# Splitting the operand transposes at the five residual boundaries of a six-block transformer kernel

## The chip, the cores and the metric

The kernel runs on one core of one Trainium2 chip, as one program with one launch. The time is the device time of an execution in microseconds (us). The profile is one execution recorded by the hardware profiler; its span runs from the first to the last instruction. The span of a profiled execution is a little shorter than its device time, because some work lies around it.

## The reference, cut to what matters

Input `x` is 256 tokens by 1024 features, float32. Six blocks follow each other, and each adds to the residual stream `h`:

```
h = x
h = h + dsa_mixer(rms_norm(h, a_attn_norm), a_w_in, ...) @ a_w_o      # tag wo
h = h + square(relu(rms_norm(h, mlp_norm[0]) @ up[0])) @ down[0]      # M0
h = h + mla_mixer(rms_norm(h, ...), latent weights w_dq, w_dkv) @ b_w_o   # B, tag bo
h = h + square(relu(rms_norm(h, mlp_norm[1]) @ up[1])) @ down[1]      # M1
h = h + (gated mLSTM and dilated attention of rmsnorm(h) @ w_in_2) @ w_out_2  # C, tag co
h = h + (silu(hf @ w_gate) * (hf @ w_up)) @ w_down,  hf = rmsnorm(h)  # F
out = rmsnorm(h, norm_final_g)
```

## The kernel before, in words

**Precision.** Every float32 operand is kept as a high part (rounded to fp32r) and a low part (the rest). The helper `three` (L546 to L550) issues three matrix products for each pair: high by high, high by low, low by high. Weights come in chunks of up to 1 MB. For each chunk c, SP loads it into one of two raw buffers, ACT makes the high part (`split_one`, L1566), and DVE (L2125) or POOL (L1535) makes the low part. There are three buffers for the parts, so ACT's split of chunk c waits until PE has finished chunk c-3 (`chunk_done`). SP's load of chunk c waits until the low part of chunk c-2 is made. Each engine has its own hand-written instruction order; semaphores tie them together.

**The boundary between two blocks.** There are five boundaries of one form: wo to M0, M0 to B, bo to M1, M1 to C, and co to F. The residual product of a block (tokens by 1024 features) fills four PSUM banks, called quarters 0 to 3: quarter = 2 * token block + feature half. Of its last chunk, PE does six products per quarter, in the order 0, 1, 2, 3 (`down_products`, L589), and closes each bank. DVE adds each quarter to `hres` (`residual_add`, L2131, instructions at L2138 and L2141). PE then turns `hres` to feature-major form with 16 transposes in four banks (`late_transposes`, L658, instruction L668): features 0 to 511 (half 0) need quarters 0 and 2, features 512 to 1023 (half 1) need quarters 1 and 3. ACT makes the high part of each of the eight feature tiles k (L1613; L1813 for B) and DVE the low part (L2151; L2402 for B). Tiles 0 to 3 come from half 0, tiles 4 to 7 from half 1. Within ACT's `late_norm`, tile k+2 waits for the low part of tile k. The next block's first products read these tiles. The scale by the root of the mean square is applied later, from squares of `hres` that ACT sums after the eight tiles (L1552).

**What stands around it.** After the products of tag wo and bo, the four quarters lie in banks 2 to 5; `mlp` waits for banks 4 and 5 to be read (`for b in (4, 5)`, L694) before its first product writes them. At M0 to B, ACT splits chunk `dkva` (L1812, `split_to("dkva")`) ahead of the first feature tile; three chunks before `dkva` stands the last down chunk of M0, whose `chunk_done` is the close of quarter 3. At M1 to C, ACT splits chunk `qm0` after the squares and roots, and DVE makes its low part next; PE needs it for `conv_tile(0)`, right after the matmuls of `C.rs` (L1151). At B, PE's first chunk (`dqa`) does nine products for each k, at C (`vm0a`) PE does token block 0 for all k and then token block 1.

```
for half in range(2):
    for blk in range(NB):
        wait_read(f"{tag}.res{2 * blk + half}")
    for odd in range(2):
        ...
```

Of the kernel before, what the change touches and what calls it, by code (L numbers as in the profile page):

```python
# [23 lines left out]
P = 128  # L24
SEQ = 256
NB = SEQ // P
D = 1024
KT = D // P
# [80 lines left out]
def program(nc, t):  # L109
# [8 lines left out]
    with ctx:  # L118
# [408 lines left out]
        def _(pe):  # L527
# [61 lines left out]
            def down_products(c, xh, xl, start, stop, closing, skip=False, base=0, quarters=(0, 1, 2, 3)):  # L589

                hi, lo = slot(c, 2, D)
                for blk in range(NB):
                    for half in range(2):
                        if 2 * blk + half not in quarters:
                            continue
                        for k in range(2):
                            ins = three(psum[:, base + 2 * blk + half, :], xh(k, blk), xl(k, blk),
                                        hi[:, k, half * 512:half * 512 + 512], lo[:, k, half * 512:half * 512 + 512],
                                        start and k == 0, stop and k == 1, skip)
                        if closing:  # L600
                            close_bank(ins, closing[2 * blk + half])
                return ins
# [24 lines left out]
            def residual(tag, x, ready):  # L627
                open_residual(tag)
                for j in range(4):
                    residual_step(tag, j, x, ready)  # L630
# [27 lines left out]
            def late_transposes(n, tag):  # L658

                for half in range(2):  # L660
                    for blk in range(NB):
                        wait_read(f"{tag}.res{2 * blk + half}")
                    for odd in range(2):
                        k0 = 4 * half + odd
                        out = open_bank(f"{n}.xT{2 * half + odd}", late_bank[n][2 * half + odd])
                        for i, k in enumerate((k0, k0 + 2)):
                            for blk in range(NB):
                                ins = nc.tensor.transpose(out[:, (2 * i + blk) * P:(2 * i + blk) * P + P],  # L668
                                                          hres[:, blk, k * P:k * P + P], ident[:, :])
                        close_bank(ins, f"{n}.xT{2 * half + odd}")  # L670
# [18 lines left out]
            def mlp(i):  # L689

                n = f"M{i}"
                late_transposes(n, ("wo", "bo")[i])
# [5 lines left out]
                def up_step(c, s_count, lo_count, j2, ready=None):  # L698
# [5 lines left out]
                    for nt in range(2):  # L704
                        out = psum[:, 4 + 2 * j2 + nt, :]
                        for k in range(KT):
                            if ready and nt == 0:
                                ready(k)
                            nc.tensor.matmul(out, hi[:, k, nt * P:nt * P + P], xA[:, :, k, :], start=k == 0, stop=False)  # L709
                            ins = nc.tensor.matmul(out[:, 0:SEQ], lo[:, k, nt * P:nt * P + P], xA[:, 0, k, :],  # L710
                                                   start=False, stop=k == KT - 1)
                    ins.then_inc(up_full, 1)

                def down_step(c, h_count, lo_count, j3, start, last):
# [3 lines left out]
                    ins = down_products(c, lambda k, blk: hb[:, 0, k, blk * P:blk * P + P],  # L718
                                        lambda k, blk: hb[:, 1, k, blk * P:blk * P + P],
                                        start, True, names if last else None, True)  # L720
                    if not last:
                        ins.then_inc(down_done, 1)
# [5 lines left out]
                up_step(c0, None, low[c0], 0, late_tile(n))  # L728
# [21 lines left out]
                down_step(c, b0 + NM, low[c], (NM - 1) % 3, False, True)  # L750

            def attention(L, logits, vcol, tag, between):
# [56 lines left out]
                for j in (2, 3):  # L809
                    product(j, (0, 1, 2, 3))  # L810
# [156 lines left out]
            late_transposes("B", "M0")  # L967
            outs = [open_bank(f"B.z{nt}", nt) for nt in range(3)]
            for part in range(2):
# [145 lines left out]


            late_transposes("C", "M1")

            def token_part(name, part, banks, ready=None):

                if part == 0:
                    for blk in range(NB):
                        open_bank(f"{name}.{blk}", banks[blk])
# [3 lines left out]
                for blk in range(NB):  # L1127
                    for k in range(4):
# [17 lines left out]
            token_part("vm0", 0, (2, 3), late_tile("C"))  # L1146
# [158 lines left out]
            residual("co", xA, lambda j: done[f"C.m{j}.lo"])  # L1305


            late_transposes("F", "co")
# [5 lines left out]
            def wide_step(c, lo_count, free_count, b, ready=None):  # L1314
# [4 lines left out]
                for nt in range(2):  # L1319
                    for k in range(KT):  # L1320
                        if ready and nt == 0:
                            ready(k)
                        ins = three(psum[:, b, nt * 256:nt * 256 + 256],
                                    hi[:, k, nt * P:nt * P + P], lo[:, k, nt * P:nt * P + P],
                                    xA[:, 0, k, :], xA[:, 1, k, :], k == 0, k == KT - 1)
# [12 lines left out]
            wide_step(c0, low[c0], None, 4, late_tile("F"))  # L1338
# [768 lines left out]
        def _(dve):  # L2107
# [709 lines left out]
```

## Time and profile before

| | us |
|---|---|
| device time, median of 3 runs | 1137.77 |
| lowest and highest of the 3 | 1137.57, 1142.76 |
| the profiled execution, device time | 1141.42 |
| its span | 1139.6 |
| PE busy (share of span) | 1112.0 (98%) |
| DVE busy | 707.6 (62%) |
| ACT busy | 583.6 (51%) |
| POOL busy | 142.6 (13%) |
| mean granted TensorE clock | 0.996 |

"Busy" of PE is the time covered by pipelined matmuls, so a slower pitch of matmuls still shows as busy; pitch is read from start to start. In a row of a timeline, "x16" merges 16 like instructions in a row, and the brackets give how long the engine was idle before and who ended that wait.

### The profile page before, as it was taken

How to read it: one execution, taken by the hardware profiler on the slowest of the kernel's cores; microseconds unless marked ns; L12 is line 12 of the kernel's file. 1: busy time of each engine (PE TensorE's matmuls, PEld its weight loads, DVE VectorE, ACT ScalarE, POOL GpSimd, SP SyncE). 2: the span in 40 equal slices, each digit the busy share in tenths (PEclk: the TensorE clock that was granted, in tenths of full speed). 3: DMA queues.
4: the chain of work that ended last, by engine and by line, in shares of the span. 5: the costliest groups of instructions: out<-in, count | busy, mean ns of one | idle time of the engine just before them, and what ended most of it. 6: DMA issues, size and time to landing. Idle time of an engine off the chain costs nothing.

```text
span 1139.6 us, 17781 instructions
## 1 busy us (share of the span) xinstructions
PE 1112.0 (98%) x7033; PEld 984.8 (86%) x7033; DVE 707.6 (62%) x997; ACT 583.6 (51%) x767; POOL 142.6 (13%) x105
## 2 busy tenths in 40 slices
PE   8899999999998999999999999999999999999997
PEld 7767888888887888888888999898899989999996
DVE  5764565565668646565656878566587566554554
ACT  5565544444579554444455546455555346443443
POOL 3543300000265240000030000000000011000001
PEclk9999999999999999999999999999999999999999
DMA  7917565555442236556545654436643545656552
GB/s 216 306 54 186 182 198 188 200 190 184 118 137 88 98 111 222 191 186 201 189 156 185 204 171 149 132 128 223 203 159 120 185 148 160 221 175 194 189 172 89
DMA packets 138782, 193.96 MB, mean 170 GB/s; under 512 B 7147, under 2 KB 112840, under 8 KB 138716
## 3 DMA queue, kind: packets, MB, share of 16 engines
q1 hardware_dynamic: 126796, 181.92, 48.4%
q10 hardware_dynamic: 11312, 11.05, 3.6%
q8 instruction: 45, 0.74, 0.3%
q0 software_dynamic: 608, 0.08, 0.1%
q14 instruction: 21, 0.17, 0.0%
HBM read 191.90 MB, written 6.37 MB: 174 GB/s over the span
## 4 chain that ended last, share of the span: by engine, by line
PE 83%; ACT 6%; DVE 5%; issue 2%; DMA 2%; POOL 0%; ACTq 0%; DVEq 0%; POOLq 0%
PE psum L548 20%; PE psum L549 20%; PE psum L550 20%; PE psum L709 11%; PE psum L710 5%; ACT arena L1552 3%; PE psum L637 2%; ACT whi L1566 2%; DVE wlo L2125 1%; DMA raw<-in_a_w_in 1%; PE psum L1264 1%; PE psum L668 1%; PE psum L1237 1%; DVE arena L2566 1%; DMA raw<-in_b_w_o 0%
## 5 line engine op out<-in xcount | busy, mean ns | idle before, releaser
L1566 ACT ACTIVATE whi<-raw 128x2048 fp32r<-128x2048 f32 (+2 forms) x174 | 325.9, 1875 | 255.5 <-PE psum L550 172.5
L2125 DVE TENSOR_TENSOR wlo<-raw,whi 128x2048 fp32r<-128x2048 f32 (+1 forms) x149 | 337.5, 2267 | 184.1 <-ACT whi L1566 183.2
L548 PE MATMUL psum<-xA,whi 128*128 128x256 f32 x840 | 239.8, 285 | 2.7 <-DVE wlo L2125 1.7
L549 PE MATMUL psum<-xA,whi 128*128 128x256 f32 x840 | 237.6, 283 | 0.0
L550 PE MATMUL psum<-xA,wlo 128*128 128x256 f32 x840 | 237.5, 283 | 0.0
L1535 POOL TENSOR_TENSOR wlo<-raw,whi 128x288 fp32r<-128x288 f32 (+3 forms) x56 | 112.6, 2037 | 793.8 <-ACT whi L1566 793.5
L709 PE MATMUL psum<-xA,whi 128*128 128x512 f32 x512 | 183.0, 400 | 0.0
L548 PEld LDWEIGHTS psum<-xA,whi 128*128 128x128 f32 x840 | 160.3, 191 | 6.0 <-DVE wlo L2125 3.2
L549 PEld LDWEIGHTS psum<-xA,whi 128*128 128x128 f32 x840 | 160.4, 191 | 0.7
L550 PEld LDWEIGHTS psum<-xA,wlo 128*128 128x128 f32 x840 | 160.4, 191 | 0.1
L548 PE MATMUL psum<-whi,xC 128*128 128x512 f32 (+1 forms) x384 | 149.2, 389 | 1.1 <-DVE xC L2439 1.1
L549 PE MATMUL psum<-wlo,xC 128*128 128x512 f32 (+1 forms) x384 | 148.6, 387 | 0.0
L550 PE MATMUL psum<-whi,xC 128*128 128x512 f32 (+1 forms) x384 | 148.1, 386 | 0.0
L710 PE MATMUL psum<-xA,wlo 128*128 128x256 f32 x512 | 143.7, 281 | 0.0
L709 PEld LDWEIGHTS psum<-xA,whi 128*128 128x128 f32 x512 | 96.2, 188 | 24.9 <-DVE xA L2151 1.2
L548 PE MATMUL psum<-whi,xA 128*128 128x512 f32 (+1 forms) x256 | 100.1, 391 | 0.0
L549 PE MATMUL psum<-wlo,xA 128*128 128x512 f32 (+1 forms) x256 | 98.6, 385 | 0.0
L550 PE MATMUL psum<-whi,xA 128*128 128x512 f32 (+1 forms) x256 | 98.6, 385 | 0.0
L710 PEld LDWEIGHTS psum<-xA,wlo 128*128 128x128 f32 x512 | 96.7, 189 | 1.1
L548 PEld LDWEIGHTS psum<-whi,xC 128*128 128x128 f32 x384 | 72.1, 188 | 16.5 <-DVE xC L2439 1.1
L550 PEld LDWEIGHTS psum<-whi,xC 128*128 128x128 f32 x384 | 72.1, 188 | 14.4
L549 PEld LDWEIGHTS psum<-wlo,xC 128*128 128x128 f32 x384 | 72.1, 188 | 12.5
(269 smaller groups left out, 1339.7 us busy)
## 6 DMA issues: line engine op xcount, KB each, us to landing
raw<-in_w_in SPq DMA_DIRECT2D x42, 1024.0 KB, 4.9
raw<-in_mlp_w_up SPq DMA_DIRECT2D x32, 1024.0 KB, 5.4
raw<-in_mlp_w_down SPq DMA_DIRECT2D x32, 1024.0 KB, 4.8
raw<-in_w_gate SPq DMA_DIRECT2D x11, 1024.0 KB, 5.1
raw<-in_w_up SPq DMA_DIRECT2D x11, 1024.0 KB, 5.2
raw<-in_w_down SPq DMA_DIRECT2D x11, 1024.0 KB, 4.8
raw<-in_a_w_in SPq DMA_DIRECT2D x6, 1024.0 KB, 7.1
raw<-in_a_w_o SPq DMA_DIRECT2D x4, 1024.0 KB, 4.7
```

The costliest lines, as they stand in the source:

```text
L548: nc.tensor.matmul(out, lh, rh, start=start, stop=False, skip_group_check=skip)
L549: nc.tensor.matmul(out, lh, rl, start=False, stop=False, skip_group_check=skip)
L550: return nc.tensor.matmul(out, ll, rh, start=False, stop=stop, skip_group_check=skip)
L637: ins = nc.tensor.transpose(out[0:m, n * P:n * P + P], src, ident[:, :])
L668: ins = nc.tensor.transpose(out[:, (2 * i + blk) * P:(2 * i + blk) * P + P], hres[:, blk, k * P:k * P + P], ident[:, :])
L709: nc.tensor.matmul(out, hi[:, k, nt * P:nt * P + P], xA[:, :, k, :], start=k == 0, stop=False)
L710: ins = nc.tensor.matmul(out[:, 0:SEQ], lo[:, k, nt * P:nt * P + P], xA[:, 0, k, :], start=False, stop=k == KT - 1)
L1237: ins = nc.tensor.matmul(psum[:, bank[f"C.h{h}.S{n}"], x * w:x * w + w], C["qa"][r0:r0 + 64, g * 4 + i, blk * P:blk * P + P], C["ka"][r0:r ...
L1535: ins = T(wlo[c % N_SPLIT][:, at:at + step], raw[c % N_RAW][:, at:at + step], f(whi[c % N_SPLIT][:, at:at + step]), ALU.subtract)
L1552: ins = nc.scalar.activation(out, in_, func, **kw)
L1566: nc.scalar.activation(whi[c % N_SPLIT][:, 0:n], raw[c % N_RAW][:, 0:n], ACT.Copy).then_inc(hi_sem, 1)
L2125: V.tensor_tensor(wlo[c % N_SPLIT][:, 0:n], raw[c % N_RAW][:, 0:n], f(whi[c % N_SPLIT][:, 0:n]), ALU.subtract).then_inc(lo_sem["dve"], 1)
```

## The change

It has three parts, at all five boundaries. PE does the quarters of the last chunk in the order 0, 2, 1, then the eight transposes of half 0, then quarter 3. DVE adds the quarters in the order 0, 2, 1, makes the low parts of tiles 0 and 1, adds quarter 3, and goes on with tile 2. PE does the next block's first products on tiles 0 and 1, then the eight transposes of half 1, then the rest; in M0, M1 and F the first step now takes both output tiles for k = 0, 1, then (after the transposes) for each further pair of k, where before it took all k of output tile 0 and then of output tile 1. At C the transposes of half 1 stand between token block 0 and token block 1 of `vm0a`, and the bank of token block 1 is opened after them. ACT's program is not touched. The core of the diff:

```diff
             def down_products(c, xh, xl, start, stop, closing, skip=False, base=0, quarters=(0, 1, 2, 3)):
 
                 hi, lo = slot(c, 2, D)
-                for blk in range(NB):
-                    for half in range(2):
-                        if 2 * blk + half not in quarters:
-                            continue
-                        for k in range(2):
...
+                for quarter in quarters:
+                    blk, half = quarter // 2, quarter % 2
+                    for k in range(2):
...
-            def residual(tag, x, ready):
-                open_residual(tag)
-                for j in range(4):
-                    residual_step(tag, j, x, ready)
+            def last_residual_step(tag, n, x, ready):
+
+                residual_step(tag, 3, x, ready, (0, 2, 1))
+                late_transposes(n, tag, 0)
+                residual_step(tag, 3, x, ready, (3,))
...
-            def late_transposes(n, tag):
-
-                for half in range(2):
...
+            def late_transposes(n, tag, half):
+
+                for blk in range(NB):
+                    wait_read(f"{tag}.res{2 * blk + half}")
...
+            def first_tiles(n, tag):
+
+                ready = late_tile(n)
+                for k0 in range(0, KT, 2):
+                    if k0 == 2:
+                        late_transposes(n, tag, 1)
+                    for nt in range(2):
+                        for k in (k0, k0 + 1):
+                            if nt == 0:
+                                ready(k)
+                            yield nt, k
...
             def mlp(i):
-                n = f"M{i}"
-                late_transposes(n, ("wo", "bo")[i])
+                n, tag = f"M{i}", ("wo", "bo")[i]
                 c0, b0 = first_of[f"mlp{i}"], i * NM
                 for b in (4, 5):
                     pe.wait_ge(read_sem[b], uses[b])
...
-                up_step(c0, None, low[c0], 0, late_tile(n))
+                up_step(c0, None, low[c0], 0, first_tiles(n, tag))
...
                 c = c0 + 2 * NM - 1
-                down_step(c, b0 + NM, low[c], (NM - 1) % 3, False, True)
+                down_step(c, b0 + NM, low[c], (NM - 1) % 3, False, True, (0, 2, 1))
+                late_transposes("BC"[i], n, 0)
+                down_step(c, b0 + NM, low[c], (NM - 1) % 3, False, True, (3,))
...
-                for j in (2, 3):
-                    product(j, (0, 1, 2, 3))
+                product(2, (0, 1, 2, 3))
+                last_residual_step(tag, "M0" if L == "A" else "M1", xA, lambda j: read[f"{L}.oT{j}"])
...
-            late_transposes("B", "M0")
             outs = [open_bank(f"B.z{nt}", nt) for nt in range(3)]
...
                     kk = 4 * part + k
+                    if kk == 2 and nt == 0:
+                        late_transposes("B", "M0", 1)
...
-            late_transposes("C", "M1")
...
-            token_part("vm0", 0, (2, 3), late_tile("C"))
+            token_part("vm0", 0, (2, 3), late_tile("C"), lambda: late_transposes("C", "M1", 1))
...
-            residual("co", xA, lambda j: done[f"C.m{j}.lo"])
-
-
-            late_transposes("F", "co")
+            open_residual("co")
+            for j in range(3):
+                residual_step("co", j, xA, lambda j: done[f"C.m{j}.lo"])
+            last_residual_step("co", "F", xA, lambda j: done[f"C.m{j}.lo"])
...
-            wide_step(c0, low[c0], None, 4, late_tile("F"))
+            wide_step(c0, low[c0], None, 4, first_tiles("F", "co"))
...
             def late_norm(n, tag, behind_low=None):
 
-                for i in range(4):
+                for i in (0, 2, 1):
                     residual_add(tag, i)
                 for k in range(KT):
+                    if k == 2:
+                        residual_add(tag, 3)
                     dve.wait_ge(*done[f"{n}.hi{k}"])
...
-            for i in range(4):
+            for i in (0, 2, 1):
                 residual_add("M0", i)
             for g, (x, v) in enumerate(((xB, V_B), (xA, V_KV))):
                 for k in range(KT):
+                    if g == 0 and k == 2:
+                        residual_add("M0", 3)
```

## Rows read from the trace of the kernel before

**Rows 1.** The page: busy time, and the chain that ended last, by engine.
```profile
PE 1112.0 (98%) x7033; PEld 984.8 (86%) x7033; DVE 707.6 (62%) x997; ACT 583.6 (51%) x767; POOL 142.6 (13%) x105
...
PE 83%; ACT 6%; DVE 5%; issue 2%; DMA 2%; POOL 0%; ACTq 0%; DVEq 0%; POOLq 0%
```
**Rows 2.** PE's timeline at wo to M0: start us, us, instruction.
```profile
121.92 2.06 PE L668 MATMUL psum<-ident,hres 128*128 128x128 f32 x16
123.73 0.48 PE L709 MATMUL psum<-xA,whi 128*128 128x512 f32 x1
...
127.33 0.40 PE L709 MATMUL psum<-xA,whi 128*128 128x512 f32 x1
```
**Rows 3.** PE's weight loads there: the second half of the transposes.
```profile
122.88 0.85 PEld L668 LDWEIGHTS psum<-ident,hres 128*128 128x128 f32 x8 [0.17 <-issue]
```
**Rows 4.** DVE's timeline there: two adds and the low parts.
```profile
120.76 0.69 DVE L2141 TENSOR_TENSOR hres<-psum,hres 128x512 f32<-128x512 f32 x1 [0.67 <-PE psum L550]
122.12 0.69 DVE L2141 TENSOR_TENSOR hres<-psum,hres 128x512 f32<-128x512 f32 x1 [0.67 <-PE psum L550]
123.06 2.73 DVE L2151 SCALAR_TENSOR_TENSOR xA<-psum,vecs,xA 128x256 fp32r<-128x256 f32 x6 [0.25 <-ACT xA L1613]
```
**Rows 5.** ACT's timeline there: a split, then the high parts.
```profile
120.23 1.92 ACT L1566 ACTIVATE whi<-raw 128x2048 fp32r<-128x2048 f32 x1 [7.00 <-DMA raw<-in_mlp_w_up]
122.56 2.66 ACT L1613 ACTIVATE xA<-psum,vecs 128x256 fp32r<-128x256 f32 x6 [0.41 <-PE psum L668]
```
**Rows 6.** PE's timeline at M0 to B.
```profile
302.39 2.12 PE L668 MATMUL psum<-ident,hres 128*128 128x128 f32 x16
304.86 0.35 PE L548 MATMUL psum<-xB,whi 128*128 128x256 f32 x1 [0.36 <-DVE xB L2402]
```
**Rows 7.** ACT's timeline at M0 to B and behind it.
```profile
302.67 1.17 ACT L1566 ACTIVATE whi<-raw 128x1152 fp32r<-128x1152 f32 x1 [2.46 <-PE psum L550]
...
304.75 1.60 ACT L1813 ACTIVATE xB<-psum,vecs 128x256 fp32r<-128x256 f32 x4 [0.19 <-DVE xB L2402]
...
309.51 1.17 ACT L1566 ACTIVATE whi<-raw 128x1152 fp32r<-128x1152 f32 x1 [0.27 <-PE psum L550]
...
313.83 0.48 ACT L1552 ACTIVATE xC<-psum,vecs 128x256 fp32r<-128x256 f32 x1 [0.50 <-PE psum L550]
```
**Rows 8.** The chain that ended last, inside block B.
```profile
320.66 1.93 ACT whi L1566
```
**Rows 9.** Timelines at bo to M1: PE twice, then DVE's last add.
```profile
415.60 0.48 PE L709 MATMUL psum<-xA,whi 128*128 128x512 f32 x1
...
419.20 0.40 PE L709 MATMUL psum<-xA,whi 128*128 128x512 f32 x1
...
413.99 0.69 DVE L2141 TENSOR_TENSOR hres<-psum,hres 128x512 f32<-128x512 f32 x1 [0.67 <-PE psum L550]
```
**Rows 10.** Timelines at M1 to C: PE three times, ACT once, DVE once.
```profile
594.20 2.12 PE L668 MATMUL psum<-ident,hres 128*128 128x128 f32 x16
596.08 0.47 PE L548 MATMUL psum<-whi,xA 128*128 128x512 f32 x1
...
607.45 0.36 PE L548 MATMUL psum<-xA,whi 128*128 128x256 f32 x1
...
594.90 0.85 ACT L1613 ACTIVATE xA<-psum,vecs 128x256 fp32r<-128x256 f32 x2 [2.45 <-PE psum L668]
...
605.03 4.50 DVE L2125 TENSOR_TENSOR wlo<-raw,whi 128x2048 fp32r<-128x2048 f32 x2 [0.94 <-ACT whi L1566]
```
**Rows 11.** PE's timeline at co to F.
```profile
943.79 0.36 PE L548 MATMUL psum<-xA,whi 128*128 128x256 f32 x1
...
947.39 0.28 PE L548 MATMUL psum<-xA,whi 128*128 128x256 f32 x1
```
**Rows 12.** Windows: PE, PEld, DVE, ACT, POOL busy, PEclk, DMA, GB/s.
```profile
0.00:10.00 10.00, 6.83 (x33) 6.34 (x33) 2.26 (x7) 3.73 (x7) 8.75 (x21) 1.00 0.85 248
10.00:20.00 10.00, 9.87 (x64) 8.91 (x65) 6.95 (x10) 7.55 (x17) 1.17 (x3) 0.83 0.69 218
...
339.00:344.00 5.00, 2.61 (x19) 2.37 (x18) 3.58 (x9) 3.18 (x8) 3.39 (x5) 1.00 0.27 90
```

More of the change, by code:

```diff
@@ L591, in down_products @@
                 hi, lo = slot(c, 2, D)
-                for blk in range(NB):
-                    for half in range(2):
-                        if 2 * blk + half not in quarters:
-                            continue
-                        for k in range(2):
[L597 to L601, printed above, removed]
+                for quarter in quarters:
+                    blk, half = quarter // 2, quarter % 2
+                    for k in range(2):
+                        ins = three(psum[:, base + quarter, :], xh(k, blk), xl(k, blk),
+                                    hi[:, k, half * 512:half * 512 + 512], lo[:, k, half * 512:half * 512 + 512],
+                                    start and k == 0, stop and k == 1, skip)
+                    if closing:
+                        close_bank(ins, closing[quarter])
                 return ins
@@ L696, in mlp, with up_step @@
                 names = [f"{n}.res{q}" for q in range(4)]
-                def up_step(c, s_count, lo_count, j2, ready=None):
+                def up_step(c, s_count, lo_count, j2, tiles=None):
                     pe.wait_ge(lo_sem[chunks[c]["lo"]], lo_count)
@@ L703, in up_step, with down_step @@
                     hi, lo = slot(c, KT, STEP)
-                    for nt in range(2):
+                    for nt, k in tiles or ((nt, k) for nt in range(2) for k in range(KT)):
                         out = psum[:, 4 + 2 * j2 + nt, :]
[L706 to L711, printed above, removed]
+                        nc.tensor.matmul(out, hi[:, k, nt * P:nt * P + P], xA[:, :, k, :], start=k == 0, stop=False)
+                        ins = nc.tensor.matmul(out[:, 0:SEQ], lo[:, k, nt * P:nt * P + P], xA[:, 0, k, :],
+                                               start=False, stop=k == KT - 1)
                     ins.then_inc(up_full, 1)
-                def down_step(c, h_count, lo_count, j3, start, last):
+                def down_step(c, h_count, lo_count, j3, start, last, quarters=(0, 1, 2, 3)):
                     pe.wait_ge(lo_sem[chunks[c]["lo"]], lo_count)
@@ L719, in down_step @@
                                         lambda k, blk: hb[:, 1, k, blk * P:blk * P + P],
-                                        start, True, names if last else None, True)
+                                        start, True, names if last else None, True, quarters=quarters)
                     if not last:
@@ L1114, in _, with token_part @@
             mlp(1)
-            late_transposes("C", "M1")
[L1119 to L1123, printed above, removed]
+            def token_part(name, part, banks, ready=None, between=None):
                 c = index[f"{name}{'ab'[part]}"]
@@ L1127, in token_part @@
                 for blk in range(NB):
+                    if part == 0:
+                        if blk and between:
+                            between()
+                        open_bank(f"{name}.{blk}", banks[blk])
                     for k in range(4):
@@ L1312, in _, with wide_step @@
             names = [f"F.res{q}" for q in range(4)]
-            def wide_step(c, lo_count, free_count, b, ready=None):
+            def wide_step(c, lo_count, free_count, b, tiles=None):
                 pe.wait_ge(lo_sem[chunks[c]["lo"]], lo_count)
@@ L1318, in wide_step @@
                 hi, lo = slot(c, KT, STEP)
[L1319 to L1325, printed above, removed]
+                for nt, k in tiles or ((nt, k) for nt in range(2) for k in range(KT)):
+                    ins = three(psum[:, b, nt * 256:nt * 256 + 256],
+                                hi[:, k, nt * P:nt * P + P], lo[:, k, nt * P:nt * P + P],
+                                xA[:, 0, k, :], xA[:, 1, k, :], k == 0 and not (tiles and nt), k == KT - 1, True)
                 ins.then_inc(gu_full, 1)
```

18 lines of the change are left out of this document (8 added, 10 removed).

## The prediction

> **What bounds the kernel now.** I read the page first. PE is busy 98% of the span and holds 83% of the chain that ended last [rows 1], so a microsecond taken from or added to PE at a boundary counts in full, unless another engine holds the chain just there. The share of busy time can't show a boundary, so next I read the five boundaries in the timelines, engine by engine, and asked two questions: how much later than its own pace does PE run, and who else stands in line behind the last product?
>
> The pace. At wo to M0 the 16 transposes start at 121.92 and the first product of M0 at 123.73, so 1.81 us, in which the second half waited 0.17 for the add of quarter 3 [rows 2, 3]. Eight transposes thus cost 0.82 to 0.9; I take 0.85. Then eight pairs of products (L709 with L710) take 3.60 us, from 123.73 to 127.33 [rows 2]. A pair at full pace takes 0.35 (one of 512 columns and one of 256, 0.23 + 0.12, which is also what later pairs take), 2.82 for eight. So 0.78 is lost to tiles that come at ACT's and DVE's pace of some 0.45 per tile (2.66 and 2.73 for six) [rows 4, 5]. The same 3.60 stands at bo to M1 [rows 9], and at co to F for eight groups of three (943.79 to 947.39) where 8 x 0.36 = 2.88 is the pace, so 0.72 [rows 11]. At M0 to B, PE loses 2.47 - 1.81 = 0.66 ahead of its first product and nothing behind it [rows 6]. At M1 to C nearly nothing is lost. **All that an earlier operand can give back is thus 0.78 + 0.66 + 0.80 + 0.72, plus the 0.17 at each of the five: some 3.8 us.**
>
> **The change, boundary by boundary.** A quarter takes 1.36 us (122.12 - 120.76, DVE's two adds, each right behind its quarter [rows 4]). Work is not added or removed: 16 transposes, 24 products, four adds, as before. The cost is in the order. Everything released by quarter 3 now comes 0.85 later, since eight transposes stand ahead of it. Everything released by the second half of the transposes comes later by the products put ahead of it.
>
> wo to M0. Transposes start at 121.92 - 1.36 = 120.56. ACT can't use that: its split runs from 120.23 to 122.15, released by a DMA [rows 5]. The first high part starts at about 122.07 instead of 122.56, DVE's low part 0.50 behind it (123.06 - 122.56 [rows 4, 5]), at 122.57, the second ends at 123.47. Only then does DVE add quarter 3, which is complete at 122.97; the add takes 0.69, to 124.16. And PE may not start M0 before it: quarter 3 of wo lies in bank 5, and `mlp` waits for banks 4 and 5 to be read. Before, that wait cost nothing, being behind the transposes. First product: 124.23, 0.50 later than before. The 0.78 of slow pairs goes, the 0.85 of the second eight transposes comes: +0.50 - 0.78 + 0.85 = **+0.6**.
>
> bo to M1. The same, but ACT is free. DVE's add starts at 413.99 + 0.85 = 414.84, ends at 415.53, first product 415.60, just as before [rows 9]: 0 - 0.80 + 0.85 = **+0.1**.
>
> co to F. Quarters lie in banks 0 to 3, the first step writes bank 4: nothing waits for quarter 3 but the second transposes. The first product starts at 943.79 - 1.81 + 0.85 = 942.83, tile 0 being ready at 942.2 by the same steps. -0.96 - 0.72 + 0.85 = **-0.8**. This is the change as one would want it.
>
> M0 to B. ACT's split of `dkva` waits for quarter 3 of M0 (released by PE at 302.67) and is put ahead of the first high part; it is in the chain [rows 7]. It starts 0.85 later, at 303.52, so the early transposes find ACT standing at a wait in front of them. The first product starts at 304.86 + 0.85 = 305.71 [rows 6], and PE idles from 303.25 to then. Two k's of nine products (18 x 0.12 = 2.16) bring it to 307.95, where the second half costs another 0.85. PE: +1.7. ACT is later still: tile 4 was made at 305.55 (third of the four from 304.75 [rows 7]) and is now at 307.95 + 0.65 = 308.6, +3.05. Waits of 0.27 and 0.50 ahead of 309.51 and 313.83 absorb some of it, which leaves 2.3. It is ACT that carries the chain from 320.66 (the split of `ukv0`), and from there it reaches PE [rows 7, 8]. **+2.3**.
>
> M1 to C. PE gains the 0.17 or so and spends it on the add of quarter 3 in front of tile 2; its arrival behind `vm0b` stays. But the second half of the transposes stands behind 12 products of 0.227: quarter 3 ends at 594.20 + 0.85 = 595.05, transposes at 597.8, tile 4's high part at 597.8 + 0.7 = 598.5 (0.7 from 594.20 and 594.90 [rows 10]), where it was at 596.7 (four times 0.40 to 0.45 behind 594.90). ACT's squares, roots and the split of `qm0` follow in order, so DVE's low part of `qm0` moves from 605.03 by 1.8 to 606.83 and ends 2.25 later, at 609.1. PE wants it at 607.4 [rows 10]. Before, the cover was 0.1 us. **+1.7**; the next chunk has 3.7 us of slack and needs nothing.
>
> The same delay of squares at M0 and M1 (some 1.8 and 1.3) ends within 0.1 of the first step's end, whose half ACT copies next: nothing, but with no cover left. SP's loads wait for low parts, so they move with these times, and no queue gets a new instruction. Interleaving k over two output tiles has no row; a switch between transposes and products has (at C 594.20 to 596.08 is 1.88 for what took 1.81 elsewhere [rows 2, 10], 0.07 each), so between 0 and 0.4 for five more switches; I take 0, since most stand behind a wait.
>
> Sum: 0.6 + 2.3 + 0.1 + 1.7 - 0.8 = +3.8 (rounded). On the profiled execution's own 1141.42 (span 1139.6 and 1.8 around it) that is 1145.2; it lies 3.65 above the median of the runs, so on the median of 1137.77 it is **1141.6**. From below, if ACT's waits absorb all that PE doesn't (B +1.7) and DVE's low part is 0.7 earlier than I place it: +2.5. From above, B at +3.05 and the switches 0.4: +5.0.
>
> **Rivals.** First, *the cover holds* (the other side): the wait that ends last at each boundary is the add and the first tiles, not a conversion queued on ACT or DVE. Then B starts on its first tile early and C's `qm0` is in time; price: -0.66 and -0.17 x 5, and the slow pairs, -3.8 at most, some -3.3 with the two bank-5 waits, 1134.5. It decides at two points: whether `dkva`'s high part can be made before quarter 3 closes, and whether `qm0`'s low part ends before 607.4. Against it: the release of ACT at 302.67 by PE [rows 7] and the 0.1 us at 607.45 [rows 10]. Chance 0.12.
>
> Second, *the clock*. B and C now have PE waits of about 2.5 and 1.7 us. In the stretch from 10 to 20 us the granted clock is 0.83 although PE is busy 9.87 of 10, behind a first stretch in which it was busy 6.83 of 10 at 1.00: 17% of 10 us, 1.7 us lost for one such fall to the lower level of 1.2 GHz. Twice that is +3.4, together +7.2: 1145.0. Against it: from 339 to 344 PE is busy 2.61 of 5 us, 2.4 idle, and the clock stays at 1.00 [rows 12]. Chance 0.04. The Trainium skill (TensorE: Matmul & The Clock Gate, Part 1) says that an array left idle falls back to 1.2 GHz and has to be kept busy to return; by that rule the new waits would be paid twice, by the row at 339 they are not.
>
> Third, *the delay grows*: with the squares and splits 1.3 to 3 us later, a load or split behind them in B or M0 arrives late once more, where B's chain runs through splits on ACT one behind the other [rows 7, 8]. One such miss of 1 to 2 us beyond the forecast: +6, 1143.8. Chance 0.14.
>
> **How the numbers follow.** Forecast 0.70 (own range +2.5 to +5.0), cover 0.12, clock 0.04, growth 0.14. The range leaves out the cover and the clock cases and little else: 1137.5 to 1145.0, which holds the spread of the runs' times too. About 0.5%, 5.7 us, is what a measurement can tell from no change. The forecast lies within; half of growth and all of the clock lie beyond: slower 0.12. Faster by 5.7 is more than all waits together: 0.02. Same 0.86.
>
> **What would show it.** Right: ACT's split of `dkva` near 303.5 and the first product of B 0.8 later behind it, a PE wait of some 2.5 us; a PE wait for `wlo` of 1.7 at `conv_tile(0)`; a wait for DVE's add ahead of M0's first product; no wait at F, whose first product follows quarter 3. Wrong: B's first product right behind quarter 3, or squares at C that end no later. The steps are wrong if the first pairs in M0 still run at 0.45.

## The result, and the profile after

| | before | after |
|---|---|---|
| device time, median (lowest to highest) of 9 runs each, us | 1141.44 (1137.57 to 1143.55) | 1147.66 (1142.40 to 1154.90) |
| ratio, 95% interval | | 1.0058 [1.003, 1.0086] |
| the profiled execution, device time and span, us | 1141.42, 1139.6 | 1147.99, 1146.2 |
| mean granted clock in it | 0.996 | 0.991 |

The changed kernel is slower by about 6.6 us (0.58%; the medians differ by 6.2). The forecast had the sign right (+3.8), but its size is below what came, and 1147.66 lies outside the range, which ended at 1145.0. A second thing moved too: the forecast stood on 1137.77 for the kernel before, the median of 3 runs, and 9 runs beside the changed kernel have 1141.44.

The page after, busy time and the chain that ended last, by engine:

```profile
PE 1114.4 (97%) x7033; PEld 988.4 (86%) x7033; DVE 707.7 (62%) x997; ACT 584.0 (51%) x767; POOL 142.6 (12%) x105
...
PE 78%; ACT 9%; DVE 7%; issue 3%; DMA 2%; POOL 1%; ACTq 0%; DVEq 0%; POOLq 0%
```

No engine has more to do than in [rows 1]: ACT's and DVE's busy time is the same within 0.4 us. But five points of the chain have gone from PE, three of them to ACT and two to DVE. That is the short form of this case: the same work, with PE standing more often behind a conversion.

PE's timeline after, wo to M0:

```profile
119.96 1.03 PE L666 MATMUL psum<-ident,hres 128*128 128x128 f32 x8
...
123.87 0.47 PE L715 MATMUL psum<-xA,whi 128*128 128x512 f32 x1 [1.50 <-DVE hres L2148]
...
125.34 1.03 PE L666 MATMUL psum<-ident,hres 128*128 128x128 f32 x8
...
136.29 0.48 PE L548 MATMUL psum<-whi,xC 128*128 128x512 f32 x1 [0.21 <-DVE xC L2228]
```

M0's first product waits for an add (L2148, the add of quarter 3, which lies in bank 5), as forecast. The last row is the first down product, at the point where the squares were to have "no cover left": it waits 0.21. ACT's timeline there shows why; the copy of the first product's half (L1641) follows the squares at once, where before ACT had stood idle for 1.23 us ahead of it:

```profile
119.99 1.92 ACT L1573 ACTIVATE whi<-raw 128x2048 fp32r<-128x2048 f32 x1 [7.35 <-DMA raw<-in_mlp_w_up]
...
130.60 0.18 ACT L1559 ACTIVATION_READ_ACCUMULATOR arena<-hres 128x1 f32 x1
130.82 0.60 ACT L1641 ACTIVATE arena<-psum 128x512 f32<-128x512 f32 x1
```

PE's timeline after, M0 to B, answering to [rows 6]:

```profile
301.45 1.03 PE L666 MATMUL psum<-ident,hres 128*128 128x128 f32 x8
...
306.17 0.36 PE L548 MATMUL psum<-xB,whi 128*128 128x256 f32 x1 [2.31 <-DVE xB L2413]
...
309.16 1.83 PE L666 MATMUL psum<-ident,hres 128*128 128x128 f32 x8
310.72 0.39 PE L548 MATMUL psum<-xB,whi 128*128 128x256 f32 x1
```

and ACT's there, answering to [rows 7]:

```profile
303.98 1.16 ACT L1573 ACTIVATE whi<-raw 128x1152 fp32r<-128x1152 f32 x1 [3.35 <-PE psum L550]
305.05 0.82 ACT L1820 ACTIVATE xB<-psum,vecs 128x256 fp32r<-128x256 f32 x2
```

The early transposes are ready at about 302.3 and ACT stands at the wait of `dkva`'s split until 303.98. B's first product waits 2.31. The rows also show something that was only a rival: the second eight transposes stand 1.56 from their start to the next product (309.16 to 310.72), while in the rows of M0 above eight of them run at the full pace. The windows (columns as in [rows 12]) say what it is:

```profile
118.00:132.00 14.00, 12.50 (x74) 10.63 (x73) 7.12 (x19) 9.29 (x19) 5.81 (x5) 1.00 0.48 163
300.00:320.00 20.00, 17.69 (x123) 16.80 (x122) 11.31 (x23) 12.12 (x25) 5.99 (x6) 0.91 0.27 79
```

In the stretch from 300 to 320 the granted clock averages 0.91; the trace has it at the lower level of 1.2 GHz from 307.4, 1.2 us after the wait of 2.31 has ended. 0.09 of 20 us is 1.8 us. The ledger below gives the price: up to its 120th product B loses 3.3 us here, and 1.75 in the three kernels that have the same wait and no fall behind it, so this fall cost 1.6. The profile has two more falls that the profiled execution of before lacks, at 331.3 and 717.0.

M1 to C (PE, then DVE) and co to F (PE), answering to [rows 10] and [rows 11]:

```profile
614.44 0.39 PE L548 MATMUL psum<-xA,whi 128*128 128x256 f32 x1 [1.67 <-DVE wlo L2132]
...
612.09 4.49 DVE L2132 TENSOR_TENSOR wlo<-raw,whi 128x2048 fp32r<-128x2048 f32 x2 [0.94 <-ACT whi L1573]
...
947.92 1.04 PE L666 MATMUL psum<-ident,hres 128*128 128x128 f32 x8
...
949.95 0.39 PE L550 MATMUL psum<-whi,xA 128*128 128x512 f32 x1
950.17 0.28 PE L548 MATMUL psum<-xA,whi 128*128 128x256 f32 x1
```

`conv_tile(0)` waits 1.67 for the low part of `qm0` (forecast 1.7). That low part starts at 612.09, in before at 605.03 [rows 10]; 5.08 of the difference is how late C was entered, so it came 1.98 later by the new order (forecast 1.8). At F the first product follows quarter 3 with no wait between, as forecast.

**The ledger.** For each kernel I took the start of the same PE instruction and subtracted its start in the profiled execution of before. What a column gains from one row to the next is what the stretch between costs. "Entering" is an instruction of the last residual product ahead of the boundary. "M0 +120" is the 120th product behind the transposes of M0, "C +60" the 60th of C, which stands behind the wait of `conv_tile(0)`.

| start minus before's, us | after | after again | undo_b | undo_c | fill_b | fill_mb | bank_map | split_later | undo_m | only_f | best2 |
|---|---|---|---|---|---|---|---|---|---|---|---|
| entering M0 | -0.60 | 0.00 | -1.41 | -3.30 | +1.52 | -3.61 | -1.89 | -4.66 | +6.75 | -3.72 | +6.77 |
| M0 +120 | +0.42 | +3.45 | +2.47 | -0.12 | +2.83 | -2.89 | -1.37 | -0.83 | +7.44 | -3.07 | +7.45 |
| B +120 | +3.73 | +6.78 | +2.45 | +1.63 | +4.51 | -1.21 | +0.38 | -1.61 | +9.19 | -3.07 | +6.65 |
| entering M1 | +4.71 | +7.84 | +3.03 | +2.67 | +5.30 | -0.59 | +1.46 | -0.38 | +10.58 | -2.99 | +6.33 |
| entering C | +5.08 | +8.20 | +3.46 | +3.06 | +5.71 | +0.06 | +0.80 | +0.02 | +10.57 | -3.01 | +5.69 |
| C +60 | +7.01 | +10.10 | +5.39 | +3.05 | +7.63 | +1.96 | +2.70 | +1.91 | +12.48 | -3.03 | +5.69 |
| entering F | +7.30 | +10.71 | +5.84 | +3.28 | +7.67 | +2.27 | +3.22 | +2.21 | +12.98 | -1.12 | +6.17 |
| end | +6.54 | +9.95 | +5.07 | +2.52 | +6.91 | +1.50 | +2.46 | +1.44 | +12.21 | -1.89 | +5.40 |

For after: -0.6 at the start, M0 +1.0, B +4.3 (to the entry of M1), M1 +0.4, C +1.9, later in C +0.3, F -0.8; together +6.5. The +0.3 is not the order's: it is what stays of the fall at 717.0, which costs PE 1.5 at first, most of it made up by 760. `fill_b`, with the new order at C and no such fall, loses 0.04 in that stretch; `before_split_later`, with the old order at C and a fall at 705.0, loses 0.70. The first row is the start-up and has nothing to do with the change: it varies from -4.7 to +6.8 over the kernels, so the end row compares single executions and the differences between rows are what I read.

### The profile page after: what moved, and what is told of

The parts are those of the page before. It is cut to its first block, busy times and chain, and to the rows that moved or that the text cites. A ratio compares the mean times of both kernels' runs of the same rounds, so it can differ in the third digit from the quotient of the medians.

```text
span 1146.2 us, 17785 instructions
## 1 busy us (share of the span) xinstructions
PE 1114.4 (97%) x7033; PEld 988.4 (86%) x7033; DVE 707.7 (62%) x997; ACT 584.0 (51%) x767; POOL 142.6 (12%) x105
## 4 chain that ended last, share of the span: by engine, by line
PE 78%; ACT 9%; DVE 7%; issue 3%; DMA 2%; POOL 1%; ACTq 0%; DVEq 0%; POOLq 0%
PE psum L548 19%; PE psum L549 19%; PE psum L550 19%; PE psum L715 9%; PE psum L716 5%; ACT arena L1559 4%; ACT whi L1573 3%; DVE wlo L2132 2%; PE psum L636 2%; POOL wlo L1542 1%; DMA raw<-in_mlp_w_up 1%; PE psum L1272 1%; DMA raw<-in_a_w_in 1%; PE psum L1245 1%; PE psum L666 1%
```

## The experiments

Each ran 7 to 12 times beside runs of before, 91 of them in all, median 1141.4. A ratio goes by the runs of before beside that kernel. The median of such a series moves with the number of clock falls in its runs, so the mean granted clock of all its runs is given where it bears on the reading. Runs of before have 0.9936 to 0.9944 in the three groups; 0.001 of 1140 us is 1.1 us, which is at most what it costs, since a fall can be made up later.

**Each boundary undone.** `undo_b`, `undo_c` and `undo_m` put back the old quarter order, sixteen transposes in a row and DVE's old order of adds, at M0 to B, at M1 to C, and at the two boundaries into `mlp`. At B:

```diff
-                down_step(c, ..., (0, 2, 1))
-                late_transposes("B", n, 0)
-                down_step(c, ..., (3,))
+                down_step(c, ...)
+                late_transposes("B", n, 0)
+                late_transposes("B", n, 1)
```

> The changed kernel with the old order at M0 to B alone (quarters 0 to 3, then 16 transposes, DVE's four adds in a row). Theory (the new PE wait at B costs 2.3 us by the order of work, and a fall of the clock on top of it, 1.7 us in the profiled run of the changed kernel): the time comes to 1.6 to 2.6 us over before, and the granted clock between 300 and 345 us is 1.00 again, mean clock 0.995 or more. Rival (the lower clock is chance of a run and has nothing to do with the wait): the time falls by 2.3 us only, to some 4 over before, and falls of the clock in block B are seen as often as with the change.

> The changed kernel with the old order at M1 to C alone. Theory (the late low part of qm0 makes PE wait 1.7 to 1.9 us at conv_tile(0)): that wait is gone, squares at C end 1.8 us earlier, the time is 1.9 us below the changed kernel, some 4.3 over before. Rival (the order at C costs nothing, the wait is made up later, since the stage behind it waits for DVE anyway): the time stays at that of the changed kernel, 6.2 over before.

> The changed kernel with the old order at wo to M0 and bo to M1. Theory (terms add up boundary by boundary: B 2.5, C 1.9, F -0.8 without falls of the clock): over before by 3.6 without falls; no fall of the clock between 118 and 132 us, since PE doesn't wait there; falls in B stay possible, so 4 to 5.5 in the median. Rival (the two boundaries cost nothing, as +0.6 and +0.1 forecast, and a fall of the clock there is chance): same time as the changed kernel, 5.7 to 6.2 over.

Measured: `undo_b` 1145.45 (ratio 1.0032 [1.0015, 1.0049]); `undo_c` 1147.06 (1.0063 [1.0038, 1.0088]); `undo_m` 1147.65 (1.0038 [1.0005, 1.007]). In the ledger the terms go where they were undone: from M0 +120 to B +120 `undo_b` gains nothing (-0.02) where after gains 3.3, and at C `undo_c` gains nothing (-0.01) where every kernel with the new order there gains 1.90 to 1.93. The times do not follow as forecast. By their ratios the three are 3.7, 7.2 and 4.3 us over before, forecast were 1.6 to 2.6, 4.3, and 4 to 5.5. `undo_b` has clock falls left at M0 (below) and at 329.2, so the clock between 300 and 345 us was not whole either. PE's rows at B in `undo_b` are those of [rows 6] again:

```profile
304.86 2.12 PE L666 MATMUL psum<-ident,hres 128*128 128x128 f32 x16
...
307.32 0.35 PE L548 MATMUL psum<-xB,whi 128*128 128x256 f32 x1 [0.35 <-DVE xB L2414]
```

`undo_c`'s median doesn't show its 1.9. The mean clock of its 7 runs is 0.9910, against 0.9926 in the first series of the changed kernel; that alone is up to 1.8 us, as much as the order gives back. Its profiled execution lost 3.2 us in M0, where after lost 1.0. PE's and ACT's timelines of `undo_b` show how:

```profile
124.37 0.76 PE L715 MATMUL psum<-xA,whi 128*128 128x512 f32 x1 [2.80 <-DVE hres L2151]
```

```profile
120.48 1.91 ACT L1576 ACTIVATE whi<-raw 128x2048 fp32r<-128x2048 f32 x1 [8.65 <-DMA raw<-in_mlp_w_up]
```

The split ahead of M0's first high parts is released by a DMA, which keeps a time of its own while PE's varies with the start-up. Here PE's transposes began at 119.16 and the split at 120.48; in after they began at 119.96 and the split at 119.99. The wait for the add is then 2.80 instead of 1.50, and the clock falls at 124.4 (window from 118 to 134, 0.89).

`undo_m` corrects the ledger: with the old order it still "loses" 0.69 in M0, and so do the other kernels with the old order there, 0.65 to 0.68. The profiled execution of before had drawn an early DMA: its split began 1.69 ahead of its transposes (120.23, 121.92), in `only_f` 0.49 ahead (117.71, 118.20). With the ordinary draw PE waits 0.40 for tile 0 in the old order too (`only_f`), where [rows 2] show none. So 0.7 of M0's +1.0 is that draw: against a run of before with the ordinary draw, after's M0 costs 0.35. The median of `undo_m` (1147.65) is that of the changed kernel, and its ratio is lower; its interval, 1.0005 to 1.007, holds both the theory and the rival. That the two boundaries cost something rests on the ledger.

**The changed kernel again.**

> The changed kernel once more, for a second profile beside the fillers. Theory (terms by order of work are the same in every run, falls of the clock vary): C +1.9, F -0.8, M1 +0.4 to within 0.1 of the first profile; M0 +1.0 or, with a fall, +3 to +4; B +2.5 or, with a fall, +4.3. Rival (the run's state changes all terms): C, M1 and F differ by more than 0.2 from the first profile.

Measured 1148.67 (1146.5 to 1158.6), ratio 1.0067 [1.0038, 1.0095]. M1, C and F are within 0.1 of the first profile (+0.36, +1.90, -0.76), M0 is +3.45 and B +4.39. Its PE shows both falls in one execution:

```profile
125.44 0.47 PE L715 MATMUL psum<-xA,whi 128*128 128x512 f32 x1 [2.47 <-DVE hres L2148]
...
127.46 1.91 PE L666 MATMUL psum<-ident,hres 128*128 128x128 f32 x8
...
309.20 0.36 PE L548 MATMUL psum<-xB,whi 128*128 128x256 f32 x1 [2.31 <-DVE xB L2413]
...
312.07 1.91 PE L666 MATMUL psum<-ident,hres 128*128 128x128 f32 x8
```

The windows of the same stretches have 0.89 and 0.93, with falls at 126.3 and 310.6:

```profile
118.00:134.00 16.00, 13.53 (x69) 11.51 (x69) 6.76 (x16) 8.18 (x18) 5.79 (x5) 0.89 0.45 153
298.00:322.00 24.00, 21.69 (x137) 19.95 (x136) 13.46 (x24) 14.72 (x26) 6.58 (x5) 0.93 0.25 74
```

**The waits filled.** To part the wait from what a fall adds, dummy products into banks that nobody reads keep PE busy while it would wait: `fill_b` 13 of 384 columns ahead of B's first product, `fill_mb` these and 6 of 512 columns ahead of M0's. Neither takes a wait away; the edit of `fill_mb` also puts its two semaphore waits ahead of M1.

```diff
                 weights(c)
+                for _ in range(13 if part == 0 else 0):
+                    nc.tensor.matmul(psum[:, 4, 0:384], hi[:, 0, 0:P], hi[:, 0, :], start=True, stop=True)
```

> The changed kernel with 13 more matmuls (128x384, into a bank that the second half of the transposes overwrites) ahead of B's first product, in PE's wait: the wait is filled, not shortened. Theory (the fall of the clock in B comes from PE standing idle there): block B runs at clock 1.00 from 300 to 345 us, B costs 2.3 to 2.5 us and not 4.3, the kernel comes to some 4 over before. Rival (the clock falls for another reason, the transposes or the stage behind): falls in B stay, and the time stays at 6.2 over before or is more.

> The changed kernel with 6 more matmuls (128x512) in PE's wait ahead of M0's first product, besides the 13 at B. Theory (the falls of the clock at M0 and at B come from PE standing idle in the waits that the change added): no fall between 118 and 132 us or between 300 and 320 us, M0 costs 0.8 to 1.3 us and B 2.5, as by the order alone; the falls from 320 us on, which the kernel before has too in some runs, stay. Rival (falls there come by chance of the run): a fall in one of the two stretches.

Measured: `fill_b` 1147.82 (ratio 1.0052 [1.003, 1.0075]), `fill_mb` 1146.09 (1.0043 [1.0023, 1.0062]). Windows of `fill_mb`:

```profile
118.00:134.00 16.00, 15.97 (x88) 13.42 (x88) 10.46 (x20) 12.14 (x22) 5.86 (x5) 1.00 0.30 91
298.00:322.00 24.00, 24.00 (x178) 23.37 (x177) 14.02 (x38) 18.18 (x37) 9.36 (x14) 1.00 0.43 130
```

The clock is whole in both stretches, B costs 2.30 (`fill_b` 2.47) from M0 +120 to the entry of M1, and M0 costs 0.72. The medians alone don't separate filled from unfilled kernels, the intervals overlap. Over all runs the mean granted clock is 0.9937 in `fill_mb` (12 runs), as in the runs of before beside it, and 0.9926 and 0.9914 in the two series of the changed kernel (9 and 8). `fill_b` has 0.9934 (8 runs) against 0.9944 beside it, and its median is no lower than that of the changed kernel: filling B alone didn't show in the time (5.9 over before by its ratio, forecast some 4). At equal clock, then, the order costs `fill_mb` 1146.09 - 1141.5 = 4.6 (4.9 by its ratio), and its profiled execution 1.50 + 3.61 = 5.1. `fill_b`'s has 6.91 - 1.52 = 5.4. Both profiles hold the 0.7 of the M0 draw. `fill_mb` has besides 0.65 at M1, where the other kernels with that order have 0.36 to 0.43; I haven't parted its own two waits from chance there.

**The suspected causes taken out one by one.** `split_later`: ACT splits `dkva` between tiles 3 and 4 instead of ahead of tile 0. `bank_map`: the quarters of wo and bo lie in banks 4, 5, 2, 3, so that M0 and M1 wait for quarters 0 and 1, not for quarter 3.

```diff
-            split_to("dkva")
             for g, (x, v) in enumerate(...):
                 for k in range(KT):
+                    if g == 0 and k == 4:
+                        split_to("dkva")
```

```diff
-res_base = {"wo": 2, "bo": 2}
+res_banks = {"wo": (4, 5, 2, 3), "bo": (4, 5, 2, 3)}
...
-    psum[:, base + quarter, :]
+    psum[:, banks[quarter], :]
```

> The changed kernel, with ACT's split of dkva moved from ahead of tile 0 of B to between tiles 3 and 4. Theory (that split, held until quarter 3 is closed, is what keeps the early transposes from being used): B's first product follows quarter 3 at once, without the wait of 2.3 us; B starts 0.8 us earlier than before and costs between -0.8 and -0.3 in all; with no such wait the clock in B stays at 1.00; the kernel comes to 1.9 to 2.5 us over before. Rival (something else holds the first tile, DVE's adds or the conversion of a weight chunk for PE): the wait shrinks by less than 1 us, or moves to the first product of dkva, and the kernel stays at 4 or more over before.

> The changed kernel with the residual quarters of wo and bo in banks 4, 5, 2, 3 instead of 2, 3, 4, 5, so that the banks M0's and M1's first step writes (4 and 5) hold quarters 0 and 1, which are added early. Theory (PE waits ahead of M0 and M1 for DVE's add of quarter 3 only because it lies in bank 5): the wait of 1.5 and 0.8 us is gone or down to 0.3, the boundaries cost -0.5 and -0.6 instead of +1.0 and +0.4, the granted clock between 118 and 132 us stays at 1.00, the kernel comes 2.5 us or more below the changed one. Rival (tiles 0 and 1 of ACT and DVE hold PE, or the add must come first anyway): the same wait stands there under DVE's low part, and the boundaries cost what they did.

`split_later` measured 1147.14 (ratio 1.0056 [1.0033, 1.0079]), with the front of B turned round: -0.78 from M0 +120 to B +120, where after has +3.3 and the kernels without a fall there +1.75. Its windows and its PE timeline:

```profile
298.00:322.00 24.00, 24.00 (x177) 23.27 (x175) 15.66 (x41) 19.98 (x40) 11.44 (x14) 1.00 0.52 159
```

```profile
300.20 1.04 PE L666 MATMUL psum<-ident,hres 128*128 128x128 f32 x8
...
304.62 1.04 PE L666 MATMUL psum<-ident,hres 128*128 128x128 f32 x8
```

PE has no wait left in 24 us, so the queue in front of ACT's first tile was the whole of B's cost there (the +1.2 up to the entry of M1 has a fall at 326.0; `best2`, which has none near, goes on at -0.3). Its time missed the forecast of 1.9 to 2.5 over before, being 5.6 over. Its profiled execution lost 3.8 in M0, with a wait of 2.73 and a fall, and the mean clock of its 12 runs is 0.9925 against 0.9944 beside it, which is up to 2.2 us; about 1 us stays open.

`bank_map` measured 1144.33, against 1140.75 in the runs beside it (ratio 1.0028 [0.9999, 1.0057]). The releaser of M0's first product changes from the add to the first low part, and the wait is 1.01, not the 0.3 or less of the forecast: M0 still costs 0.52, forecast -0.5, since ACT's split stands ahead of the tiles. From the entry of M1 to that of C it gains 0.66 where after loses 0.37. PE's timeline at M0:

```profile
122.09 0.47 PE L715 MATMUL psum<-xA,whi 128*128 128x512 f32 x1 [1.01 <-DVE xA L2160]
```

The split of `dkva` alone, put later in the kernel of before (`before_split_later`, the same edit with all sixteen transposes together), asks whether it is worth anything there:

> The kernel before, with ACT's split of dkva behind tile 3 of B, and nothing else. Theory (in the kernel before, that split alone puts the first tile behind PE): the first product of B follows the 16th transpose, 0.66 us are gained at B and nothing anywhere else, 0.3 to 0.8 below before. Rival (the split then holds the later tiles or dkva's own low part): 0 or over.

The time can't tell: 1140.25, ratio 0.9998 [0.9981, 1.0015], which is 2 us either way. The trace can. The first product follows the 16 transposes after 1.87, where before took 2.47, and from M0 +120 to B +120 the kernel gains 0.59:

```profile
298.45 2.12 PE L668 MATMUL psum<-ident,hres 128*128 128x128 f32 x16
300.32 0.36 PE L548 MATMUL psum<-xB,whi 128*128 128x256 f32 x1
```

So the split in front of tile 0 held PE in the kernel of before too, and 0.6 of what `split_later` gains at B needs no new order of the transposes.

**What is left that gains.** `only_f` is the kernel before with the change at co to F alone. `best` is the changed kernel with `bank_map`, `split_later` and the old order at C. `best2` is `best` with the old order also at wo to M0.

> The kernel before with the change at co to F alone. Theory: the first product of F follows quarter 3 at once, the boundary gives 0.76 us, no wait is added anywhere, mean clock as before (0.994 to 0.995): 0.5 to 1.0 below before. Rival (order is not what gains or costs, placement of the new code is): over before by 1 or more.

> The changed kernel with the banks of bank_map, the later split of dkva of split_later, and the old order at C. Theory (each wait that the change added had one cause of its own, and with the causes gone the early operand pays): M0 -0.5, M1 -0.6, B -0.8 in front and 0 to -0.8 at its end, C 0, F -0.8: 2.0 to 3.5 below before without falls of the clock, and no fall at M0 or in the first part of B. Rival (the gains at PE are eaten by the squares that ACT now makes later, ahead of the first step's copy, and by block B's own chain on ACT): -0.8 to -1.5 in all.

> The kernel 'best' with the old order at wo to M0 too, so new order at M0 to B (dkva's split later), bo to M1 (quarters in banks 4, 5, 2, 3) and co to F. Theory (at wo to M0 ACT's split, released by a DMA, keeps the early transposes from being used, so the order there can only cost): M0 0, B -0.8 in front, M1 -0.7, C 0, F -0.8: 2.2 below before where no clock falls, and lower than 'best' by 0.5 to 1. Rival (nothing is gained past F): 0.8 below before, the same as only_f.

| | median (lowest to highest), us | ratio to before |
|---|---|---|
| only_f | 1138.76 (1136.88 to 1140.63) | 0.9966 [0.9939, 0.9992] |
| best | 1139.55 (1136.62 to 1142.15) | 0.996 [0.993, 0.9989] |
| best2 | 1137.35 (1134.22 to 1147.59) | 0.9968 [0.9942, 0.9993] |

All three beat both kernels by their intervals and can't be told apart; that `best2` would be 0.5 to 1 below `best` isn't shown. F gives -0.77 in `only_f`, as in every kernel that has it. The rest of its 2.0 to 3.9 (median, ratio) is no effect of the order that any row shows: its runs have a mean clock of 0.9958 against 0.9936 beside them, up to 2.5 us. `best` and `best2` have 0.9942 and 0.9944 against 0.9936 and 0.9937, up to 0.8. The profiled execution of `best` has M0 at +1.15 with a wait of 1.64, forecast -0.5, and M1 at -0.66 and F at -0.77. At wo to M0 the new order gained nothing clear in any kernel: the 0.52 of `bank_map` is 0.15 below what the old order takes with the ordinary draw. In `best2` the stretch M0 +120 to entering M1 gives -1.1, M1 -0.6 and F -0.8, -2.5 in all (0.5 of it goes again late in C, with a fall at 714.4). That is three quarters of the -3.3 of the first rival, 0.6 of it by the later split alone: the gain is there once nothing is queued behind the last product.

## Why the prediction was right or wrong

**Right: sign, places and mechanisms.** Every wait that it named stands where it named it. M0's first product waits for the add of quarter 3. `dkva`'s split starts at 303.98 (forecast 303.52, the whole execution being 0.4 late by then), the first product of B waits 2.31 (forecast 2.5), `conv_tile(0)` waits 1.67 (forecast 1.7), F gives 0.76 (forecast 0.8). B's PE part was forecast at +1.7 and is 1.75 where no fall follows the wait. The first rival, that the cover holds, is out by the rows that it named. The third, a load or split that is late once more by 1 to 2 us, doesn't show: behind B +120 the order costs 0.8 up to M1 (`fill_b`; the forecast had 0.6 there), and no other stretch between two boundaries grows by more than 0.25 where no clock falls.

**Wrong, before any mechanism: the base.** The prediction saw that the profiled execution (1141.42) lay 3.65 above the median of 3 runs (1137.77), and put its +3.8 on the latter: 1141.6. Two of those 3 runs were among the fastest of before; 9 runs have 1141.44. On that base the same +3.8 gives 1145.2, and the upper bound of the range, 7.2 above its base, would have held the measured 6.2 to 6.6. So of the 6.1 us between forecast and measurement, 3.7 is the base and 2.4 is the change. The size of the change was still too small, for the two reasons below.

**Wrong, first: the step "the clock", priced rightly and given 0.04.** The price was 1.7 us for a fall. The profiled execution has one behind B's new wait, 1.6 to 1.8 us, and so B cost 4.3; without it the same order costs 2.8 to 3.1 there (`undo_c`, `bank_map`, `undo_m`), and 2.3 to 2.5 with the wait filled. The second profile has two. The step that failed is the evidence against it: one window in which PE had idled 2.4 of 5 us at 1.00 [rows 12] was read as "waits of this size don't lower the clock". That window is a single wait:

```profile
343.76 1.06 PE L637 MATMUL psum<-ident,arena 128*128 128x128 f32 x8 [2.39 <-DVE arena L2487]
```

One stretch that stays at 1.00 doesn't say that the next will. Over all profiles, for the places with a new PE wait:

| place | wait, us | falls right behind it |
|---|---|---|
| M0 | 2.18, 2.47, 2.73, 2.80 | 4 of 4 |
| M0 | 1.01, 1.50, 1.64, 1.80 | 0 of 4 |
| B | 2.31 (same in all) | 2 of 5 |
| C, `conv_tile(0)` | 1.67 to 1.69 | 0 of 8 |
| M0 or B, filled, undone or cause removed | none over 0.5 | 0 |

and for two places in B where PE waits in either order:

| place | wait, us | falls |
|---|---|---|
| near 344 in before's time (`before`, `fill_b`, `best2`) | 2.39, 2.39, 2.23 | 0 of 3 |
| near 326 in before's time (all 14 profiles) | 1.06 to 1.72 | 11 of 14, in the wait or up to 1.2 us behind it |

The rule of the Trainium skill (TensorE: Matmul & The Clock Gate, Part 1), that an idle array falls back to 1.2 GHz and has to be kept busy to return, stood beside that sentence as a single clause; the runs go with it in direction (falls behind the longer new waits, none where they are filled). The length of a wait alone doesn't decide: 2 of 5 at B and 0 of 3 near 344 had waits of over 2.2 us, and near 326 shorter ones were enough, with the old order as well (3 of 4 kernels with the old order at B fall there). Ten of the kernels have one at 705 to 721 as well, behind no wait of over 0.9 us. That the new waits cause the falls at M0 and B is supported by the profiles, not proven: no kernel with a shorter wait or none falls at either place, six of nine with a wait over 2.1 do. It rests on fourteen profiled executions.

**Wrong, second: small terms, nearly all from below.** The order alone was forecast at +3.8; the profile of `fill_b` has 5.4, that of `fill_mb` 5.1, the runs of `fill_mb` 4.6.

- M0, +0.6 forecast: +1.0 (`fill_mb` 0.7, `fill_b` 1.3). Of after's, about 0.2 is the first down product, which waits 0.21 for the squares' sake. The prediction had said that they end within 0.1 of what follows and priced it at nothing; with 0.1 of cover and a shift of 1.8 that was a term and not a remark. Another 0.7 is the DMA-released split, which the prediction took at the one place where the profile of before had it: it is a draw that differs from run to run, and the early one had been read as the rule. Over the six kernels with this order and the old banks M0 runs from +1.0 to +3.9, mean 2.8, of which four have a fall.
- M1, +0.1: +0.37, with the same 0.2 wait ahead of the first down product.
- C, +1.7: +1.9, since `qm0`'s low part comes 1.98 later and not 1.8. The wait of 1.67 is the same thing counted from the end of the product before; starts are 1.9 later, and nothing is lost ahead of it. The 0.3 later in the block is the fall at 717.0.
- B, +2.3: +2.3 to +2.5 with the wait filled, 2.8 to 3.1 with the wait open and no fall behind it. The open ones all have the fall near 326, `fill_b` none; I haven't parted the two.

**The sum.** Against the profile of before, after's order costs 1.0 + 0.4 + 2.5 + 1.9 - 0.8 = 5.0, and its falls the rest of the 7.1 from the entry of M0 on: about 1.8 in B and 0.3 in C. Against the runs, the M0 draw has to come off and the falls go in by their share. M0 is then 2.8 - 0.7 = 2.1 (six profiles), B 3.5 (the mean of its five profiles with the open wait), M1 0.4, C 1.9, F -0.8: 7.1, an estimate from those single executions, where the two series measured +6.6 and +7.6 by their ratios. The forecast's own upper end, +5.0, left out the clock, and the range's, 1145.0, was set at the price of the whole of that rival.

## What to carry to other kernels

Splitting an operand so that its first half is ready early only pays if nothing stands in the consumers' queues behind the last product: look for conversions, sums and bank reads that wait for it, and move those first (`split_later` turned the first 120 products of B from +1.75 to -0.8, `bank_map` M1 from +0.4 to -0.7). Where a new order gives TensorE a wait of about the size of those here, add a clock fall (some 1.7 us) to its price with a real chance: 6 of the 12 waits from 2.18 to 2.80 us behind the start-up had one. Don't take a single stretch that stayed at full clock as evidence against it. Put the forecast on a base of more than three runs where they differ by more than the change. Take a start that a DMA releases as a range, since PE's own time slides against it from run to run.

## What the runs showed of the hardware that was not expected

- The start-up alone moves the entry of M0 by -4.7 to +6.8 us between profiled executions. A part of it is the clock's falls in the first 50 us: before has two (10.8 and 38.1 us), `fill_b` one (36.3), `only_f` none; the two latest kernels there, `undo_m` and `best2`, have two longer ones each.
- The same wait of 2.31 us at B was followed by a fall in two profiles and not in three. A fall can be made up later: the one at 717.0 cost 1.5 us at first and 0.3 at the entry of F. For M0 the falls began between 0 and 1.1 us after the wait had ended, for B 1.2 and 1.4.
- At the lower level (1.2 GHz) eight transposes of 128x128 float32 take 1.56 us from their start to the next product, at full clock 0.79, so here they took twice as long at half the clock.
